# Scratch stores split by head, the values' copy ahead of the last rotary's low part, and another share of adds between GpSimd and VectorE in the norms of a three-layer transformer step

## The reference, cut to what matters

```python
def first_block(x, c, positions, ...):                 # 2 layers: grouped attention, sink attention
    for i in range(DEPTH):
        sh1, sc1, g1, sh2, sc2, g2 = jnp.split(silu(c) @ ada_w[i] + ada_b[i], 6, axis=-1)
        h = modulate(rms_norm(x, norm_g[i, 0]), sh1, sc1)
        y = nsa_mixer(h, ...) if i % N_MIXERS == 0 else swa_sink_mixer(h, ...)
        x = x + (1 + g1)[:, None, :] * rms_norm(y, norm_g[i, 1])
        h = modulate(rms_norm(x, norm_g[i, 2]), sh2, sc2)
        y = squared_relu_mlp(h, mlp_w_up[i], mlp_w_down[i])
        x = x + (1 + g2)[:, None, :] * rms_norm(y, norm_g[i, 3])
    return x

def swa_sink_mixer(h, w_in, w_out, sinks, cos, sin):
    q, k, v = jnp.split(h @ w_in, [qd, qd + kd], axis=-1)
    q, k = apply_rope(q, cos, sin), apply_rope(k, cos, sin)
    return banded_attention(q, k, v, SWA_WINDOW, sinks) @ w_out

def second_block(x, mem, ...):
    x = x + hybrid_mixer(rms_norm_2(x, norm_mix_w), ...)
    x = x + memory_cross_attention(rms_norm_2(x, norm_xattn_w), rms_norm_2(mem, norm_mem_w), ...)
    x = x + conv_ffn(rms_norm_2(x, norm_ffn_w), ...)
    return rms_norm_2(x, norm_final_w)
```

## Time and profile before

| | us |
|---|---|
| median of 3 runs | 2206.26 (2205.83 to 2215.26) |
| the profiled execution | 2207.97 |
| its span | 2206.2 |
| TensorE busy | 2019.4 (92%) |
| VectorE busy | 1232.0 (56%) |
| GpSimd busy | 965.2 (44%) |
| ScalarE busy | 697.7 (32%) |

### The profile page before, as it was taken

How to read it: one execution, slowest core, us unless ns; L and a number is a source line. 1 busy time by engine, 2 the same in 40 slices (tenths; PEclk the granted TensorE clock), 3 DMA queues, 4 the chain that set the end, 5 groups by cost and what they waited for, 6 DMA issues and landing times.

```text
span 2206.2 us, 26660 instructions
## 1 busy us (share of the span) xinstructions
PE 2019.4 (92%) x10136; PEld 1649.7 (75%) x10136; DVE 1232.0 (56%) x1734; ACT 697.7 (32%) x1217; POOL 965.2 (44%) x547
## 2 busy tenths in 40 slices
PE   6989999799999989588999999799898699999997
PEld 5868777678888868576888888588678377888886
DVE  7574776974564786458442537775322326536264
ACT  3333554322222332443222223323333123222222
POOL 1455554445445444554444444342336034444442
PEclk9998999899999999798999999899999699999999
DMA  6655332345545305321333333121224022323231
GB/s 272 205 191 177 106 91 107 122 172 172 191 172 198 137 29 190 125 77 53 104 98 100 96 96 96 48 87 48 96 77 153 1 75 69 96 96 97 94 97 66
DMA packets 78664, 252.15 MB, mean 114 GB/s; under 512 B 10840, under 2 KB 11352, under 8 KB 78296
## 3 DMA queue, kind: packets, MB, share of 16 engines
q1 hardware_dynamic: 78552, 250.61, 34.3%
HBM read 235.21 MB, written 15.37 MB: 114 GB/s over the span
## 4 chain that ended last, share of the span: by engine, by line
PE 69%; DVE 12%; issue 8%; POOL 4%; DMA 4%; ACT 2%; SPq 1%; DVEq 0%; POOLq 0%; ACTq 0%
PE ps L872 18%; PE ps L874 18%; PE ps L873 18%; POOL wl L772 3%; PE ps L1113 2%; DMA qscr<-rot_ls 2%; PE ps L1056 2%; PE ps L1085 2%; DMA qscr<-rot_l 1%; PE ps L1363 1%; POOL pr L793 1%; SPq L622 1%; ACT pr L2371 1%; PE ps L1340 1%; PE ps L935 1%
## 5 line engine op out<-in xcount | busy, mean ns | idle before, releaser
L772 POOL TENSOR_TENSOR wl<-raw,wh 128x1024 fp32r<-128x1024 f32 x309 | 778.1, 2522 | 1060.5 <-ACT wh L2235 1060.5
L2235 ACT CAST wh<-raw 128x1024 fp32r<-128x1024 f32 x309 | 323.1, 1050 | 1046.8 <-PE ps L874 934.3
L872 PE MATMUL ps<-ah,wh 128*128 128x512 f32 x1336 | 525.1, 393 | 2.1 <-POOL wl L772 2.1
L873 PE MATMUL ps<-ah,wl 128*128 128x512 f32 x1336 | 521.3, 390 | 0.0
L874 PE MATMUL ps<-al,wh 128*128 128x512 f32 x1336 | 521.2, 390 | 0.0
L872 PEld LDWEIGHTS ps<-ah,wh 128*128 128x128 f32 x1336 | 251.9, 189 | 57.3 <-issue 4.7
L873 PEld LDWEIGHTS ps<-ah,wl 128*128 128x128 f32 x1336 | 251.6, 188 | 53.4 <-issue 1.5
L874 PEld LDWEIGHTS ps<-al,wh 128*128 128x128 f32 x1336 | 251.6, 188 | 52.8
L872 PE MATMUL ps<-hh,wh 128*128 128x512 f32 x688 | 271.8, 395 | 7.7 <-DVE hl L1884 3.9
L874 PE MATMUL ps<-hl,wh 128*128 128x512 f32 x688 | 270.3, 393 | 0.0
L873 PE MATMUL ps<-hh,wl 128*128 128x512 f32 x688 | 269.4, 392 | 0.0
(11 more groups left out here) (344 smaller groups left out, 2826.7 us busy)
## 6 DMA issues: line engine op xcount, KB each, us to landing
raw<-in_units SPq DMA_DIRECT2D x309, 512.0 KB, 3.5
ada_mlp<-in_ada SPq DMA_DIRECT2D x64, 512.0 KB, 3.3
ada<-in_ada SPq DMA_DIRECT2D x16, 512.0 KB, 16.1
qs<-qscr SPq DMA_DIRECT2D x32, 256.0 KB, 3.4
ada_in<-in_ada SPq DMA_DIRECT2D x16, 512.0 KB, 3.7
ks<-kscr SPq DMA_DIRECT2D x24, 256.0 KB, 5.0
x<-in_xT SPq DMA_DIRECT2D x1, 2048.0 KB, 13.2
qscr<-rot_h SPq DMA_DIRECT2D x8, 256.0 KB
```

Of the source, the lines that this page charges most:

```text
L772: nc.gpsimd.tensor_tensor(wl[:, slot], raw[:, slot], wh[:, slot].bitcast(F32), ALU.subtract).then_inc(lo_done, 1)
L872: nc.tensor.matmul(out_ap, wh[:, slot, k], high[:, k0 + k], start=first and k == 0, stop=False)
L873: nc.tensor.matmul(out_ap, wl[:, slot, k], high[:, k0 + k], start=False, stop=False)
L2235: a.copy(wh[:, slot], raw[:, slot]).then_inc(hi_done, 1)
```

## The change

**Stores.** Each result's high and low part is stored with one DMA for each head, 128 KB from 32 partitions (both halves of the head dimension) in place of 256 KB from 128 partitions; `ROTS`, the number of stores for each result, goes from 4 to 8. `pair_c` goes out in four DMAs in place of two, `vtmp` likewise. In SyncE's queue, at the last units of the second projection stage (`ks<-kscr` and `qs<-qscr` are loads of the attention's first heads, `raw` a weight unit, `rot_hs` and `rot_ls` the high and low part of one result, `qscr` the scratch), this stands before:

The diff, cut to its core; of `store_k`, which is changed as `store_q`, and of the functions that were only moved nothing is shown:

```diff
-ROTS = (4,) * 11
+ROTS = (8,) * 11
...
         if n - plan.nth0 >= 4:
             eng.wait_ge(pv_made, plan.after_work(n - 4)[1])
+        elif not plan.nsa and n - plan.nth0 < 2:
+            eng.wait_ge(rot_made, 11)
         elif not plan.nsa:
             for index in (9, 10):
                 eng.wait_ge(rot_kept[index % 2], rot_count(index))
...
         def store_q(index, grp):
             sp.wait_ge(rot_made, index + 1)
             for low_part, rot in enumerate((rot_high_of(index), rot_low_of(index))):
-                for half in range(2):
-                    row = 64 * low_part + 32 * half
-                    sp.dma_start(qscr[4 * grp:4 * grp + 4, row:row + 32], rot[:, half].bitcast(F32)).then_inc(rot_kept[index % 2], 16)
+                for j in range(4):
+                    sp.dma_start(qscr[4 * grp + j, 64 * low_part:64 * low_part + 64].rearrange("(a r) t -> r a t", a=2),
+                                 rot[32 * j:32 * j + 32].bitcast(F32)).then_inc(rot_kept[index % 2], 16)
...
         sp.wait_ge(kc_made, 1)
-        for half in range(2):
-            sp.dma_start(cscr[0, :, 32 * half:32 * half + 32], pair_c[:, 2 * half]).then_inc(kc_kept, 16)
+        for g in range(GROUPS):
+            sp.dma_start(cscr[0, g].rearrange("(a r) t -> r a t", a=2),
+                         pair_c[32 * g:32 * g + 32, 0:4:2]).then_inc(kc_kept, 16)
...
-            sp.dma_start(cscr[1, 2 * n:2 * n + 2], vtmp[:, n]).then_inc(vc_kept, 16)
+            for i in range(2):
+                sp.dma_start(cscr[1, 2 * n + i], vtmp[64 * i:64 * i + 64, n]).then_inc(vc_kept, 16)
...
         def added_norm(n, name, shift=True):
-            add_odd(n, 1)
-            add_odd(n, 3)
+            add_scaled(n, 1)
+            add_scaled(n, 2)
             low_of_norm(name, shift, 1)
-            add_odd(n, 5)
+            add_scaled(n, 3)
+            add_scaled(n, 4)
             low_of_norm(name, shift, 3)
-            add_odd(n, 7)
+            add_scaled(n, 5)
+            add_scaled(n, 6)
             low_of_norm(name, shift, 5)
...
             def scaled(c):
                 if c == 0:
                     dve.wait_ge(spread, stds[0])
-                if factor and c % 2:
-                    dve.wait_ge(x_new_pool, x0 + c // 2 + 1)
+                if factor and 1 <= c <= POOL_ADDS:
+                    dve.wait_ge(x_new_pool, p0 + c)
                 elif factor:
-                    dve.wait_ge(x_new, x0 + c // 2 + 1)
+                    dve.wait_ge(x_new, x0 + 1 + (c > 0))
...
-                add_even(0)
-                add_odd(1)
+                add(0)
                 scaled(0)
-                add_even(2)
-                add_odd(3)
+                to_add(1)
                 low(0)
+                to_add(2)
+                to_add(3)
                 scaled(1)
+                to_add(4)
                 scaled(2)
-                add_even(4)
-                add_odd(5)
+                to_add(5)
                 low(2)
                 scaled(3)
+                to_add(6)
                 scaled(4)
-                add_even(6)
-                add_odd(7)
+                add(7)
                 low(4)
...
-        def rotary(to, whole=False, query=False):
+        def rotary(to, whole=False, query=False, last=False):
...
+            if last:
+                return
+            rotary_low(to, query)
+
+        def rotary_low(to, query):
             index = rots[0]
...
                     dve.wait_ge(v_turned, 1)
                     v.tensor_copy(vv[:, 0, :, 0:P], ps[:, 5].rearrange("p (i f) -> p i f", i=SC)).then_inc(v_placed, 1)
+                    rotary_low(pair_s, query=True)
...
-        for _ in range(4):
-            rotary(pair_s, query=True)
+        for p in range(4):
+            rotary(pair_s, query=True, last=p == 3)
         v.tensor_copy(v_t[:], bank()).then_inc(evac, 1)
...
+        def highs_and_squares(u, out_t, bank0, factor=None):
+            for c in range(DC):
+                if c < DC - 1:
+                    highs(u + RING + c, u + RING + c + 1)
+                else:
+                    a.activation(warm[:], eps[:], ACT.Sqrt)
+                squares(out_t[:, c:c + 1], (evac, lambda _: bank0 + c + 1), count=1,
+                        added=6 * summed[0] + max(c - 2, 1) if c >= 2 else None)
+                if c == DC - 1:
+                    root(0 if factor else 1)
+                if factor:
+                    a.activation(wt[:, c % 2], out_t[:, c], ACT.Square, scale=factor(c)).then_inc(w_made, 1)
+            highs(u + RING + DC - 1, u + RING + DC)
+            summed[0] += 1
+            if factor:
+                root_of_new()
```

More of the change, by code:

```diff
@@ L533, in build @@
     POOL_LOWS = (1, 3, 5)
+    POOL_ADDS = 6
     A_READY, n_dve, n_pool = {}, 0, 0
@@ L611, in store_k @@
             for low_part, rot in enumerate((rot_high_of(index), rot_low_of(index))):
-                for half in range(2):
-                    sp.dma_start(kscr[branch, :, low_part, 32 * half:32 * half + 32],
-                                 rot[:, half].bitcast(F32)).then_inc(rot_kept[index % 2], 16)
+                for g in range(GROUPS):
+                    sp.dma_start(kscr[branch, g, low_part].rearrange("(a r) t -> r a t", a=2),
+                                 rot[32 * g:32 * g + 32].bitcast(F32)).then_inc(rot_kept[index % 2], 16)
         def store_q(index, grp):
@@ L682, in _ @@
         sp.wait_ge(kc_made, 1)
-        for half in range(2):
-            sp.dma_start(cscr[0, :, 32 * half:32 * half + 32], pair_c[:, 2 * half]).then_inc(kc_kept, 16)
+        for g in range(GROUPS):
+            sp.dma_start(cscr[0, g].rearrange("(a r) t -> r a t", a=2),
+                         pair_c[32 * g:32 * g + 32, 0:4:2]).then_inc(kc_kept, 16)
         units(10, 11)
-        sp.wait_ge(kc_kept, 32)
+        sp.wait_ge(kc_kept, 16 * GROUPS)
         load_tokens(0)
@@ L809, in attention, with add_scaled @@
                     centre(w)
-        def add_odd(n, c):
-            pool.wait_ge(u_made, DC // 2 * n + c // 2 + 1)
+        def add_scaled(n, c):
+            pool.wait_ge(u_made, POOL_ADDS * n + c)
             nc.gpsimd.tensor_tensor(x[:, c], y[:, c], x[:, c], ALU.add).then_inc(x_new_pool, 1)
@@ L1439, in norm_shared, with add, to_add @@
             inv = ps[:, 5]
-            def add_even(c):
+            def add(c):
                 u = ps[:, (b0 + 2) % RING]
-                if c:
-                    dve.wait_ge(x_new, x0 + c // 2)
                 link(v.scalar_tensor_tensor(out=u, in0=y[:, c], scalar=factor(c), in1=ps[:, 4], op0=ALU.mult, op1=ALU.mult))
                 v.tensor_tensor(x[:, c], u, x[:, c], ALU.add).then_inc(x_new, 1)
-            def add_odd(c):
+            def to_add(c):
                 v.scalar_tensor_tensor(out=y[:, c], in0=y[:, c], scalar=factor(c), in1=ps[:, 4],
@@ L2251, in squares @@
                 squared[0] += 1
-        def highs_and_squares(u, out_t, bank0, factor=None):
-            for c in range(DC):
-                highs(u + RING + c, u + RING + c + 1)
-                if c == DC - 1:
-                    a.activation(warm[:], eps[:], ACT.Sqrt)
-                squares(out_t[:, c:c + 1], (evac, lambda _: bank0 + c + 1), count=1,
-                        added=6 * summed[0] + max(c - 2, 1) if c >= 2 else None)
-                if factor:
-                    a.activation(wt[:, c % 2], out_t[:, c], ACT.Square, scale=factor(c)).then_inc(w_made, 1)
-            summed[0] += 1
         def root(slot, tokens=S):
@@ L2427, in _ @@
         n += 8
-        root(0)
-        root_of_new()
         highs_of_norm(ah, coef_at(0, 4), n=n)
@@ L2522, in _ @@
         n += 8
-        root(1)
         highs_of_norm(ah, n=n)
```

4 lines of the change are left out of this document (2 added, 2 removed).

## The result

| | us |
|---|---|
| before, median (four runs) | 2207.14 (2205.83 to 2215.26) |
| changed, median (four runs) | 2183.66 (2175.63 to 2187.43) |
| ratio, 95% interval | 0.9881, 0.9844 to 0.9918 |
| the changed kernel's profiled execution, its span | 2175.63, 2173.8 |

The account below looks back on a forecast made before the run. TensorE was 69% of the chain, with losses where it waits behind 12 to 15 us rotary stores. −16 − 12.5 + 6.8 + 5.2 − 3.6 = −20.1 us, from median 2206.26 to 2186, range 2175 to 2198 (8 in 10).

Parts of the forecast that it names:

- The store: Rotary result stores: split by head they spread over the DMA engines at 250 GB/s, landing in about 7 us, not 13.
- Rival A: Rotary stores do not spread, a batch stays at 13 us and SyncE issues twice as much: 2212 us; chance 0.05.
- First stage −12.5: First projection stage: quicker stores end TensorE's standing, lost clock and ScalarE's waits for weight loads: −12.5 us, bounds −6 and −16.
- the 2 us left over: First projection stage: 2 us of TensorE's 14.4 us loss were left as not recovered.
- Rival C: First stage gains half, since VectorE's rotary and GpSimd's low parts bind: −6 us in place of −12.5, 2193; chance 0.20.
- Second attention −16: Second attention's entry: earlier `v_t` and quicker stores let the third work begin 16.3 us earlier: −16 us, bounds −12 and −19.
- Start of the norms with an add +6.8: Four norms' start: VectorE's small two-SBUF-input operations are held until GpSimd's low part is done: +6.8 us, bounds −1 and +9.
- Rival B: Norms' start: VectorE is not held, so +6.8 becomes 0 and the whole 2179 us; chance 0.14.
- Body +5.2: Body of the four norms with an add: GpSimd's row grows from 7 to 9 operations: +5.2 us, bounds −2 and +8.
- one more 0.3: Norm body: chunks behind the sixth follow at TensorE's pace with 0.3 us more, ending +1.4.
- xq and ffn −3.6: Norms of xq and ffn: last square no longer waits behind cast and table load, 1.8 us each: −3.6, bounds −4 and −1.5.
- ±1 of `pair_c` and `vtmp`: Splitting these stores, four more issues beside weight units already loaded: 0 us, bounds −1 and +1.

Follow-up runs that it names:

- S alone: Kernel before with only the stores by head (both attentions' results, `pair_c`, `vtmp`), values' copy and norms as before: 2177.81 us, ratio 0.9871.
- V: Values' copy ahead of the last low part, first two works waiting for `rot_made` 11 alone; by itself on the kernel before: 2208.35 us, ratio 1.0001.
- A alone: Kernel before with only ScalarE's new order at the last chunk (last cast behind the square and table load): 2215.45 us, ratio 1.0035.
- The experiment with PSUM: Changed kernel with `new_sum`'s running value in PSUM in place of SBUF from its second operation on: 2175.03 us, ratio 0.9858 against before.
- N alone: Kernel before with only the new share of adds in the four norms with an add: 2211.49 us, ratio 1.0017.
- S, V, A and the PSUM sum: Changed kernel with the norms' share of adds of before and `new_sum`'s running value in PSUM: 2171.57 us, ratio 0.984; again 2171.15 us, 0.9825.
- S, V and A together: Kernels with stores by head, the values' part and ScalarE's new order, among them the changed kernel: 2183.66 us, ratio 0.9881 against before.
- S and A without V: Adds of before and PSUM sum, with stores by head and ScalarE's order but without the values' part: 2174.08 us, ratio 0.9832 against before.

## Why the prediction was right

- **The store.** Right in mechanism: the share went from 0.26 to 0.91, at 245 GB/s over 4 us where 250 was taken. The issue, taken at 0.57 to 0.63 us, took 0.45, and a result was landed in about 6 us in place of 7. "DMA: Bandwidth & Descriptors" of the Trainium skill, section on why a DMA increments its semaphore by 16 and not by 1, gave this outcome, and this case's traces agree. The loss that follows from "Door 1: The DMA port swizzle" in "SBUF — State Buffer" of the Trainium skill (189 GB/s for 32 partitions) did not come: 245 GB/s were measured, with stores of several heads under way at once; one alone was not measured. Rival A is out.
- **First stage −12.5:** measured −12.1 and −12.5, with the 2 us left over about what TensorE still stands (2.7). The clock's part of the sum was too small: 0.05 of the 63.25 us busy would be 3.2 and not 3.7, while the traces show 4.4 (389 matmuls in 63.25 us before, 392 in 59.33 now). Rival C (half of it) is out: VectorE's rotary and GpSimd held TensorE for 1.5 and 1.2 us, once each.
- **Second attention −16:** measured −17.4. The size is right, but the walk took the copy's move as a part of it (881.5 + 5.0 + 1.2). With S alone the low part is not late either, and the same 17.4 comes; no worth of V shows in either company. That the walk's sum came out near is in part luck: it left out that the low part's wait would go by itself, and added the move that takes its place. The step asked what the copy had waited for, and not whether that wait would still be there once the stores were quick.
- **Start of the norms with an add +6.8:** 1.9, 1.7, 0.3 and 1.7 by the first scalings in the trace, 5.6, and the same 5.6 with A alone, whose four stages come to 6.2. Rival B is out: 128 columns are held as 512 are. The experiment with PSUM showed the cause, which was until then only read from durations.
- **Body +5.2:** N alone 3.9; in the changed kernel the four norms cost 11.1 in all, 5.5 behind the start. With N alone in swa_in the first chunk is 1.65 us earlier and the sixth 1.1 us later, both as laid out, and the stage ends at that +1.1: the "one more 0.3" behind did not come. Each of the other norms is 0.3 to 0.4 less, too. What the layout by hand lacked is the wait of the first scaled chunk for the spread of the new root (0.85 us idle at 802.13); before, another chunk's operations stood in front of it. In mlp0 and swa_in this wait is there in the changed kernel and not with N alone, since the later root finds TensorE at half clock: twice 0.75 us, about the difference of 5.5 and 3.9. So the size is right by two errors that cancel.
- **xq and ffn −3.6:** −6.0 in the traces. The wait of 1.8 us between chunk and square went down to 0.03 us in both. Besides, TensorE had not yet lost full clock when it spread the root (1.16 us for the eight matmuls in both norms, 1.79 and 2.08 before), which the step had not counted. How much of the rest is the change's is open, since xq and ffn also move by −0.9 and −1.2 with N alone.
- **The sum** was right by terms of which the largest error is 2.4 us. Together the same stages give −24.4 in place of −20.1; first attention (−3.1, −0.5) and cross attention (−4) stood in no term. The ratio 0.9881 means a gain of 26 us and the medians one of 23.5, where 20 was forecast. The bounds of the steps add up to −42 and −2.5 (without the ±1 of `pair_c` and `vtmp`) and not to −41 and −4, which moves no stage's forecast.

## What to carry to other kernels

A store with few rows in its slowest dimension can be slow whatever the bytes: here 4 rows gave a share of 0.26, and 32 rows 0.91. Look for a DMA share that is a simple fraction of 16 engines, and cut the transfer so that it spreads, but no finer, since each issue took 0.45 us of the queue here. Before an instruction is moved in front of another's wait, ask whether the change beside it does away with that wait. When work is moved to GpSimd or its start is moved, look at what VectorE does in those microseconds with two inputs in SBUF: either move it or put one operand into PSUM.

## What the runs showed of the hardware

Executions of one kernel lie in a band of 3 to 17 us (the changed one: 2175.63 to 2187.43, before in one series of 23 runs: 2203.74 to 2216.55). In the traces most of this sits in three stretches, and in each it is a stretch of granted half clock more or less: the first attention (from −3.1 to +4.9 us against before over the traces), the mixer (0, +1.2 or +3.9) and the cross attention. The kernel with S, V, A and the PSUM sum was traced twice. In the first attention, the same 84 matmuls, first trace and second:

```profile
242.80:255.80 13.00, 11.42 (x84) 9.03 (x86) 10.54 (x27) 6.24 (x18) 6.03 (x10) 1.00 0.18 52
```

```profile
245.00:261.40 16.40, 14.76 (x84) 10.92 (x86) 10.65 (x27) 6.35 (x19) 6.14 (x10) 0.79 0.14 44
```

This is the execution's and not the kernel's. Of the 6.2 us between these two executions (2168.8 and 2174.98 us) 3.8 lie in the first attention and 2.1 in the first stage; the cross attention is the same in both (−3.8, −3.7).

The cross attention, before and the changed kernel, the same work:

```profile
1700.00:1770.00 70.00, 48.59 (x114) 24.91 (x112) 22.70 (x70) 12.10 (x44) 0.00 (x0) 0.66 0.03 8
```

```profile
1675.60:1740.70 65.10, 43.59 (x115) 22.62 (x113) 22.58 (x70) 12.23 (x44) 0.00 (x0) 0.74 0.03 9
```

The clock is 0.66 in the one and 0.74 in the other, and 5 us are saved in this stretch, the 4 us of the table over the whole stage. So it stood in all six traces of kernels with S, V and A together (−3.7 to −4.0), and in none of the seven others (from −0.4 to +0.9, and +2.0 with S and A without V). That speaks for the kernel and against the execution, though nothing was changed in this stage; a reason for it is not on record.

By the mean granted clock the changed kernel's eight runs fall in two groups: 0.960 and 0.961 (2175.63, 2178.61 and 2178.8 us), and 0.954 to 0.956 (2182.3 to 2187.43 us). Both traced ones are of the first. The first trace lies 6.4 us under the mean of the eight runs (2182.0), so of its −32 some 6 us are likely the execution's, an estimate from these runs; in which stretch the slower group loses them was not shown, since none of its executions was traced.
